# Weights that land where their low parts will stand: two rings of six chunks in place of three of four

## The reference

```python
ada = (silu(c) @ w_ada + b_ada).reshape(b, 9, 1, 2048)        # w_ada 2048 x 18432
h = rmsnorm(x, g_ffn1) * (1 + sc1) + sh1
x = x + 0.5 * gt1 * ((silu(h @ w1_gate) * (h @ w1_up)) @ w1_down)   # 2048 x 5632, 5632 x 2048
h = rmsnorm(x, g_mix) * (1 + sc2) + sh2
x = x + gt2 * (token_mix(h @ w_in) @ w_out)                   # 2048 x 6144, 2048 x 2048
h = rmsnorm(x, g_ffn2) * (1 + sc3) + sh3
x = x + 0.5 * gt3 * ((silu(h @ w2_gate) * (h @ w2_up)) @ w2_down)
return rmsnorm(x, g_final)
```

## Time and profile before

| What | Value |
| --- | --- |
| median of three executions | 1909.04 us |
| the profiled execution, its own time | 1909.02 us |
| span in its trace (first to last instruction) | 1907.2 us |
| TensorE busy | 1865.6 us (98%) |
| VectorE busy | 1310.6 us (69%) |
| ScalarE busy | 849.6 us (45%) |
| mean granted TensorE clock | 0.991 of full speed |
| HBM read | 503.10 MB, 265 GB/s over the span |

### The profile page before, as it was taken

The page is one execution under the profiler, slowest core; times in us unless marked ns, Lnnn a source line. Parts: engine busy times, 40 slices in busy tenths (PEclk is TensorE's granted clock), DMA queues, the critical chain, the costliest instruction groups (busy, mean ns, idle before and its releaser), DMA issues. The chain is left out here.

```text
span 1907.2 us, 21163 instructions
## 1 busy us (share of the span) xinstructions
PE 1865.6 (98%) x8392; PEld 1542.6 (81%) x8392; DVE 1310.6 (69%) x1357; ACT 849.6 (45%) x969; POOL 0.2 (0%) x4
## 2 busy tenths in 40 slices
PE   5899999999999999999999999999999999999998
PEld 4688888888888888788887887888888888888886
DVE  6898887888778888776665677666655454444454
ACT  6444444334444444644543546444443334444443
POOL 0000000000000000000000000000000000000000
PEclk7999999999999999999999999999999999999999
DMA  9898899889888888686454575777765555556554
GB/s 388 357 398 345 317 369 365 342 331 352 338 334 333 339 331 304 225 333 243 154 174 146 179 253 177 284 280 280 262 214 187 194 188 201 184 192 213 189 191 140
DMA packets 117889, 506.61 MB, mean 266 GB/s; under 512 B 13728, under 2 KB 13984, under 8 KB 98464
## 3 DMA queue, kind: packets, MB, share of 16 engines
q1 hardware_dynamic: 117792, 505.27, 72.1%
HBM read 503.10 MB, written 2.12 MB: 265 GB/s over the span
## 5 line engine op out<-in xcount | busy, mean ns | idle before, releaser
L831 DVE TENSOR_TENSOR w_lo<-w_raw,w_hi 128x1024 fp32r<-128x1024 f32 x652 | 794.9, 1223 | 501.9 <-ACT w_hi L635 501.0
L635 ACT CAST w_hi<-w_raw 128x1024 fp32r<-128x1024 f32 x652 | 684.5, 1051 | 989.3 <-PE banks L1095 930.5
L1093 PE MATMUL banks<-w_hi,x_split 128*128 128x512 f32 x1776 | 701.8, 395 | 10.6 <-DVE x_split L956 10.6
L1095 PE MATMUL banks<-w_hi,x_split 128*128 128x512 f32 x1776 | 693.7, 391 | 0.0
L1094 PE MATMUL banks<-w_lo,x_split 128*128 128x512 f32 x1776 | 692.8, 390 | 0.0
L1093 PEld LDWEIGHTS banks<-w_hi,x_split 128*128 128x128 f32 x1776 | 334.7, 188 | 80.0 <-issue 11.8
L1095 PEld LDWEIGHTS banks<-w_hi,x_split 128*128 128x128 f32 x1776 | 334.3, 188 | 70.9
L1094 PEld LDWEIGHTS banks<-w_lo,x_split 128*128 128x128 f32 x1776 | 335.0, 189 | 67.5
L1093 PE MATMUL banks<-w_hi,hidden 128*128 128x512 f32 x704 | 274.3, 390 | 0.0
L1095 PE MATMUL banks<-w_hi,hidden 128*128 128x512 f32 x704 | 273.9, 389 | 0.0
L1094 PE MATMUL banks<-w_lo,hidden 128*128 128x512 f32 x704 | 273.9, 389 | 0.0
(11 more groups left out here) (132 smaller groups left out, 605.7 us busy)
## 6 DMA issues: line engine op xcount, KB each, us to landing
w_raw<-w_chunks SPq DMA_DIRECT2D x656, 512.0 KB, 4.2
ada_raw<-w_ada_tiles SPq DMA_DIRECT2D x112, 1024.0 KB, 5.9
ada_early<-w_ada_tiles SPq DMA_DIRECT2D x32, 1024.0 KB, 8.9
gate_row<-gate_rows SPq DMA_DIRECT2D x3, 1024.0 KB, 5.9
residual<-x_t SPq DMA_DIRECT2D x2, 1024.0 KB, 8.8
out_t<-residual SPq DMA_DIRECT2D x4, 512.0 KB, 3.1
table<-tables SPq DMA_DIRECT2D x1, 1664.0 KB, 9.6
cond_row<-g_final_t SPq DMA_DIRECT2D x1, 1024.0 KB, 5.3
```

The costliest lines, as they stand in the source:

```text
L635: nc.scalar.copy(w_parts(c)[0], raw[:, c % RING, :]).then_inc(hi_ready, 1)
L831: nc.vector.tensor_tensor(lo, raw[:, c % RING, :], hi.bitcast(F32), ALU.subtract).then_inc(lo_ready, 1)
L1093: nc.tensor.matmul(o, x_hi, hi, start=(first and k == k0), stop=False, skip_group_check=True)
L1095: ins = nc.tensor.matmul(o, x_lo, hi, start=False, stop=(last and k == k0 + KC - 1), skip_group_check=True)
```

## The change

`w_raw` is no longer a ring of its own: it is an alias of `w_lo`. The DMA lands in the place where the low part will stand, ScalarE reads it from there, and VectorE subtracts in place. The memory of the third ring makes the two others longer: six places each (2 x 6 = 12, as 3 x 4 before). So the rounding of chunk c no longer waits for a place that its DMA did not already have; the DMA of chunk c now waits for `w_free` of chunk c - 6. The loops still run four chunks ahead (AHEAD = 4), so the order of the instructions on ScalarE and VectorE stays. The extra places behind the norms and all that belongs to them are gone.

```diff
-RING = 4
+RING = 6
+AHEAD = 4
...
-ADA_FROM = FIRST * (PART + SLICES) - RING
+ADA_FROM = FIRST * (PART + SLICES) - AHEAD
...
-def ring():
...
-    extra = {NORM_AT[n] + 1 + i: RING + i for n in (1, 2) for i in range(2)}
...
-SLOT, BEFORE = ring()
...
-        raw = sb("w_raw", [P, RING, CH])
...
-        whx = nc.alloc_sbuf_tensor_at("w_hi_ahead", [P, 2, CH], F32R, offset=late_at)
-        wlx = nc.alloc_sbuf_tensor_at("w_lo_ahead", [P, 2, CH], F32R, offset=late_at + 2 * CH * 4)
+        landing = nc.alloc_sbuf_tensor_at("w_raw", [P, RING, CH], F32, offset=low + HID_BYTES + DT * 2 * T * 4 + RING * CH * 4)
...
-            at = SLOT[c]
-            return (whi[:, at, :], wlo[:, at, :]) if at < RING else (whx[:, at - RING, :], wlx[:, at - RING, :])
+            return whi[:, c % RING, :], wlo[:, c % RING, :]
+
+        def raw(c):
+
+            return landing[:, c % RING, :]
...
                 if c >= RING:
-                    sp.wait_ge(lo_ready, c - RING + 1)
-                sp.dma_start(raw[:, c % RING, :], w_all[c]).then_inc(raw_in[c % RING], 16)
+                    sp.wait_ge(w_free, c - RING + 1)
+                sp.dma_start(raw(c), w_all[c]).then_inc(raw_in[c % RING], 16)
...
-            for c in range(RING):
+            for c in range(FIRST):
                 w_chunk(c)
...
-                elif kind == "w" and n >= RING:
+                elif kind == "w" and n >= FIRST:
...
                 at = ADA_AT[i] + 8
-                for n in (1, 2):
-                    if ADA_AT[i] < NORM_AT[n] < ADA_AT[i + LATE]:
-                        at = NORM_AT[n] + 12
...
-                    if c - 12 in (NORM_AT[1], NORM_AT[2]):
-                        sp.wait_ge(w_free, c - 12 + 3)
...
                 act.wait_ge(raw_in[c % RING], 16 * (c // RING + 1))
-                if BEFORE[c] is not None:
-                    act.wait_ge(w_free, BEFORE[c] + 1)
-                if SLOT[c] >= RING:
-                    act.wait_ge(ada_step, ada_done(c))
-                nc.scalar.copy(w_parts(c)[0], raw[:, c % RING, :]).then_inc(hi_ready, 1)
+                if c >= RING:
+                    act.wait_ge(w_free, c - RING + 1)
+                nc.scalar.copy(w_parts(c)[0], raw(c)).then_inc(hi_ready, 1)
...
-            for c in range(ADA_FROM - RING, CHUNKS):
-                if c + RING < CHUNKS:
-                    w_hi(c + RING)
+            for c in range(ADA_FROM - AHEAD, CHUNKS):
+                if c + AHEAD < CHUNKS:
+                    w_hi(c + AHEAD)
...
-                nc.vector.tensor_tensor(lo, raw[:, c % RING, :], hi.bitcast(F32), ALU.subtract).then_inc(lo_ready, 1)
+                nc.vector.tensor_tensor(lo, raw(c), hi.bitcast(F32), ALU.subtract).then_inc(lo_ready, 1)
```

More of the change, by code:

```diff
@@ L1078, in _ @@
                         stage[name](n)
-                if c + RING < CHUNKS:
-                    w_lo(c + RING)
+                if c + AHEAD < CHUNKS:
+                    w_lo(c + AHEAD)
         @block.tensor
```

## The result

The kernel after took 1912.32 us in the median of 20 executions (1910.52 to 1914.04), the kernel before on the same chip 1909.07 (20 executions, 1908.61 to 1910.71). The ratio is 1.0016 with a 95% interval of 1.0010 to 1.0023: 3.25 us slower, inside the 0.2% named as what can be told from no change. Forecast were 1912.1 us and "within". The profiled execution took 1911.98 us, with a span of 1910.2 us. One execution of a later run, e3_no_extra, took 2709.57 us at a mean granted clock of 0.655 and is left out of that run's ratio, though not of its median.

A forecast was written before the change was run, and what follows sets the result against it. TensorE was taken to bound the kernel, busy 1865.6 of 1907.2 us. Main loop 0, two inner norms at 1.55 and opening 0 gave 3.1 us on top of 1909.02, so 1912.1 us, range 1909.0 to 1916.3.

The forecast's parts named there:

- Norms: Two inner norms: chunk n + 3's DMA flight delays rounding, `modulate` and first split, +1.55 us each.
- the sum: Whole kernel: main loop 0, two norms at 1.55 us and opening 0 make 3.1 us slower.
- The waits at a norm: TensorE at each inner norm: 1.3 us for `x_split`, 1.2 for `normed`; waits sum to 2.95 instead of 1.4 us.
- a few tenths: Inner norms: chunks n + 1 and n + 2 land before their turn but for this, in front of a TensorE wait.
- Opening: Opening: chunks 20 and on 2.9 us late, made up by about 121 us; 0 us, at most 2.9.
- the second rival: Opening does not catch up: chunks 30 to 44 arrive 2.9 us later; up to 2.9 us, 1915.0; chance 0.15.
- Main loop: Main loop: same instructions, landings covered by five chunks, 13.3 us; 0 us, at most some 3.
- the third rival: Middle: longest landings meet a group's end, +3 us, 1915.1; chance 0.14, shared with norm landings near 4.4 us.
- The prediction's own sign of being wrong: Anywhere in the kernel: the forecast is wrong if TensorE waits for `w_lo`; no such wait was expected.
- Rival 1: Inner norms: the clock falls after idling, 1.6 us a fall, 6.3 in all, 1915.3; chance 0.11 alone or with others.
- limit near 3.5 us: Inner norms: idle time at a norm near which the clock's fall was said to decide.
- Rivals 4 and 5: Norms' loss hidden, 1909.0 to 1910, chance 0.12; VectorE ahead in the opening, faster by over 3.8 us, chance 0.03.

The follow-up runs named there:

- e3_no_extra: Kernel before without its extra places, three rings of four: median 1920.60 us, ratio 1.0059 to before.
- e1: Kernel before with the DMAs of chunks n + 3 and n + 4 held back at both inner norms as in the change: 1911.88 us, ratio 1.0013.
- e2: Kernel after with two extra places in the memory of `ada_raw` for chunks n + 3 and n + 4: 1910.83 us, ratio 1.0006 to before.
- e9: Kernel after with the extra places of chunks n + 1 and n + 2 kept as before had them: 1910.61 us, ratio 1.0004 to before.
- e11: Kernel after with roundings of chunks n + 3, n + 4 and the low part of n + 3 put later at the inner norms: 1911.26 us, ratio 1.0012.
- e5: Kernel after run again unchanged, as control in the second job: 1912.25 us, ratio 1.0015 to before.
- e6: e2 with the w_ada tile in front of chunk 64 issued one chunk earlier: 1910.12 us, ratio 1.0004 to before.
- e7: Kernel after with the w_ada tile in front of chunk 64 issued one chunk earlier: 1911.89 us, ratio 1.0013 to before.
- e8: Kernel after with one further 512 KB DMA ahead of that of chunk n + 3 at both inner norms: 1917.28 us, ratio 1.0038 to before.
- e10: e9 with the w_ada tile behind chunk 63 moved to behind chunk 62: 1910.43 us, ratio 1.0003 to before.
- e12: e10 with w_ada tiles 32 and 33 issued behind chunks 44 and 46: 1910.15 us, ratio 1.0003 to before.

## Why the prediction was right

- **Norms, 1.55 us each.** The mechanism was as forecast, link by link from the issue to the first split; shown by e1 (the late DMAs alone bring it), e2 and e9 (an earlier release takes it away) and e11 (another order takes away some 40%). The sizes were 1.25 and 1.43, in e5 1.28 and 1.20. Against before, and without the 0.24 us by which this trace was late already, the first split came 1.40 us later at the second norm: 776.31 - 774.67 - 0.24. At the third it was 1168.03 - 1164.98 - 1.49 = 1.56. From the split to `normed` it takes 4.11 us where it took 4.24: the chain gave back 0.13, and the sum had it at nothing. At the second norm the landing was 3.2, not 3.3.
- **The waits at a norm, 2.95 us.** They were 2.5 and 2.9. At the second norm the idle time ahead of the last wait (0.5, as before) came in three pieces, 0.39, 0.76 and 0.85, not in two of 1.3 and 1.2. Part of it moved ahead, into the tail: chunks n + 1 and n + 2 were "a few tenths" late, as the forecast said, but not "in front of a wait for TensorE" alone. The first residual went from 769.26 to 770.62, 1.12 us beyond the shift, behind their low parts. The trace of e6 shows what that part costs with a landing of 4.7 us: some 1.05 us. In e5 it cost nothing: both norms had one wait of 1.4 us for the split and the two for `normed`, 2.7 us in all.
- **Opening, 0.** Right in the profiled execution of after. Chunk 18's DMA left at 82.0, the moment named (82.02), the lag was down to 0.4 us at chunk 32 (landed at 127.4 us) and the landings of 120 to 156 us took 7.2 in the median against 7.1. The waits for the split input are 10.1 against 10.6. In e5, e7 and e11 the second rival came true in small: 1.7 to 2.0 us of the lag stayed, at a price of 0.42, 0.19 and 0.14 us at chunk 44, not 2.9.
- **Main loop, 0.** Right in the profiled execution of after, a little low over many: the third rival in small. Its place was named (a long landing at a group's end on VectorE), its price of 3 us was far too high. A single spot at chunk 64 did it, at 1.3 us in e5. The prediction's own sign of being wrong, "if TensorE waits for `w_lo` anywhere", stands in that trace: 1.08 us at 231.71. By that sign its 0 for the main loop does not hold for every execution of this kernel. The longest landing from 300 to 750 us even fell from 10.1 to 7.3 us.
- **The clock.** Rival 1 did not come true: the granted clock stays at 1.00 from 770 to 790 us. Its mechanism is real, as e8 shows behind 2.85 us and e3 behind 4.30. Its price of 1.6 us a fall was 0.5 us net at one norm of e8 and 1.7 at the other. Its argument against itself ("each gap is shorter than the one that did no harm", 2.24 us) rested on one execution: in the opening of e11 the matmuls behind a wait of 2.12 us lasted 0.63 us (last section). So that the clock stayed up behind the 1.59 us of the third norm agrees with every other trace here with pieces up to 1.6 us at a norm, but no limit near 3.5 us can be read from the runs.
- **Rivals 4 and 5.** Not so: the interval ends above 1.

Of the measured 3.25 us the norms are 2.68 in the profiled execution of after and 2.48 in e5's. The sum had 3.1 for them, and nothing for the other 0.6 to 0.8. That the total came within 0.2 us of the forecast is therefore partly luck: a term some 0.5 us too high and terms at nothing that were not quite nothing met. The two places outside the norms (chunks 44 and 67) cost 0 us in after's trace and 1.75 in e5's, so the rest may well lie there; the median's share of it was not measured. The start-up also differs from one execution to the next: at chunk 13 the shift lies between -1.33 us (e7) and +1.09 (e1), which would be enough too; that was not tested.

## What to carry to other kernels

If a transfer lands in the place where its result will stand, its issue waits for the last reader of that place, and its whole flight (3.2 to 3.4 us for 512 KB here, with the queue empty) falls behind that release. Count, at each spot where the consumer frees places late, whether the ring is deep enough to hold flight and both passes: depth six cost 3 us here, nearly all of it at two such spots; depth five cost 30, of which some 17 there and the rest in the opening and the middle. Where it isn't deep enough, look first at what stands in fixed order behind the landing. And where a delay makes one longer idle piece on TensorE, look at the granted clock as well: it fell here behind single pieces from 2.12 us on, though not behind every one, and in e8 it made 2.8 us of delay cost 5.0.

## What the runs showed of the hardware

- At the norms, one idle piece of 2.85 us on TensorE was followed by matmuls of 0.63 us instead of 0.39 (e8), while pieces of 1.6 and 0.9 us at one norm were not. The size of a piece alone does not tell, though. In the openings 2.24 us did no harm and behind 3.48 the clock fell, but the same wait, some 77.6 us into the span, shows the reverse in two other traces. First e7, then e11:

```profile
77.65 0.47 PE L1069 MATMUL banks<-w_hi,x_split 128*128 128x512 f32 x1 [3.27 <-DVE x_split L932]
77.96 0.39 PE L1070 MATMUL banks<-w_lo,x_split 128*128 128x512 f32 x1
```

```profile
77.60 0.65 PE L1077 MATMUL banks<-w_hi,x_split 128*128 128x512 f32 x1 [2.12 <-DVE x_split L937]
78.05 0.63 PE L1078 MATMUL banks<-w_lo,x_split 128*128 128x512 f32 x1
```

From 77.6 to 81.0 us the granted clock is 1.00 in e7 and 0.52 in e11. The Trainium skill's "TensorE: Matmul & The Clock Gate", Part 1, says that the gate falls after idling; e8 and e11 agree, and e7 shows that it need not fall behind 3.27 us. Whether splitting the idle time is what kept the clock up at the norms of after is not shown: its largest piece was 1.6 us, and no trace falls behind a piece that short.
- In e8 the chunk's DMA, issued 0.37 us behind the extra one of the same size, landed 4.3 us after its own issue, where 3.2 stood in after with an empty queue: the transfer in front cost it 1.1 us at the second norm and 1.0 at the third (4.4 in place of 3.4).
- The last store of 512 KB took 3.6 us to land in eleven traces and 4.2 in e9, e10 and e12, where one packet of instructions moved in the same stretch. The cause is not shown.
